# Both key/value heads of one branch in a prompt attention unit, with its matmul pairs in two halves of the array

## The reference

```python
# group B, per query block of 128 (w: sliding window, s: selected, c: compressed)
s_w = einsum('bqhgd,bkhd->bqhgk', q, kb) * SCALE          # h: 2 kv heads, g: 4 query heads of each
e, m, l = masked_exp(s_w, okw)
o_w = einsum('bqhgk,bkhd->bqhgd', normalise(e, l), vb)
out = g[..., 0] * o_c + g[..., 1] * o_s + g[..., 2] * o_w
```

## Time and profile before

| what | value |
| --- | --- |
| three runs, us | 1436.48, 1436.84, 1442.02 |
| the profiled execution, us | 1435.87 |
| its span, us | 1434.1 |
| mean granted PE clock | 0.947 of 2.4 GHz |
| PE busy | 1321.0 us, 92% of the span |
| DVE, ACT busy | 802.1 us (56%), 520.5 us (36%) |
| attention units, layer 0 and 1 | 363.7 to 452.2 us, 1060.2 to 1148.6 us |

### The profile page before, as it was taken

How to read it: one execution, slowest core, us unless ns; L and a number is a source line. 1 busy time by engine, 2 the same in 40 slices (tenths; PEclk the granted TensorE clock), 3 DMA queues, 4 the chain that set the end, 5 groups by cost and what they waited for, 6 DMA issues and landing times.

```text
span 1434.1 us, 24304 instructions
## 1 busy us (share of the span) xinstructions
PE 1321.0 (92%) x9753; PEld 1163.5 (81%) x9753; DVE 802.1 (56%) x1483; ACT 520.5 (36%) x762; POOL 118.4 (8%) x207
## 2 busy tenths in 40 slices
PE   5999997999998989999799999799899987999993
PEld 4999996656775789999799999766477666999992
DVE  5555546774665265554565544577547545555433
ACT  3333335410453263333353333334025434333321
POOL 9000002012000010000200000200120001000001
PEclk9999998997899989999989999899969998999996
DMA  8555577447164336646735546764632631565540
GB/s 260 180 181 167 148 209 256 144 147 244 46 176 119 93 110 185 190 132 162 217 121 178 175 132 173 237 240 133 206 127 73 163 117 60 177 187 167 155 108 30
DMA packets 251909, 226.81 MB, mean 158 GB/s; under 512 B 11716, under 2 KB 234066, under 8 KB 249634
## 3 DMA queue, kind: packets, MB, share of 16 engines
q1 hardware_dynamic: 245282, 204.08, 48.1%
q0 software_dynamic: 6528, 21.37, 4.3%
HBM read 221.55 MB, written 3.86 MB: 157 GB/s over the span
## 4 chain that ended last, share of the span: by engine, by line
PE 84%; DVE 9%; ACT 3%; issue 2%; DMA 1%; SPq 1%; POOL 0%; DVEq 0%
PE bank L746 21%; PE bank L747 21%; PE bank L748 21%; PE bank L665 9%; PE bank L855 3%; PE bank L1012 2%; PE bank L755 1%; PE bank L933 1%; PE bank L756 1%; PE bank L883 1%; PE bank L835 1%; DVE bc_pages L1656 1%; ACT x L1227 1%; DVE rstd L1755 1%; DVE w_low L1510 1%
## 5 line engine op out<-in xcount | busy, mean ns | idle before, releaser
L746 PE MATMUL bank<-x_high,w_low 128*128 128x264 f32 x1408 | 406.1, 288 | 27.6 <-DVE x_low L1492 23.3
L747 PE MATMUL bank<-x_low,w_high 128*128 128x264 f32 x1408 | 403.1, 286 | 0.0
L748 PE MATMUL bank<-x_high,w_high 128*128 128x264 f32 x1408 | 402.6, 286 | 0.0
L1510 DVE TENSOR_TENSOR w_low<-weights,w_high 128x2048 fp32r<-128x2048 f32 (+1 forms) x172 | 347.7, 2039 | 69.5 <-ACT w_high L1206 55.9
L746 PEld LDWEIGHTS bank<-x_high,w_low 128*128 128x128 f32 x1408 | 268.8, 191 | 31.6 <-issue 27.9
L747 PEld LDWEIGHTS bank<-x_low,w_high 128*128 128x128 f32 x1408 | 269.8, 192 | 0.0
L748 PEld LDWEIGHTS bank<-x_high,w_high 128*128 128x128 f32 x1408 | 268.3, 191 | 0.0
L746 PE MATMUL bank<-hidden_high,w_low 128*128 128x264 f32 x704 | 205.0, 291 | 0.0
L748 PE MATMUL bank<-hidden_high,w_high 128*128 128x264 f32 x704 | 199.8, 284 | 0.0
L747 PE MATMUL bank<-hidden_low,w_high 128*128 128x264 f32 x704 | 199.2, 283 | 0.0
L1248 ACT ACTIVATE w_high<-weights 128x2048 fp32r<-128x2048 f32 (+1 forms) x88 | 163.9, 1862 | 8.2 <-DMA weights<-in_ffn_wu_dram 8.2
(11 more groups left out here) (302 smaller groups left out, 1686.8 us busy)
## 6 DMA issues: line engine op xcount, KB each, us to landing
weights<-in_ffn_wg_dram SPq DMA_DIRECT2D x44, 1024.0 KB, 5.5
weights<-in_ffn_wu_dram SPq DMA_DIRECT2D x44, 1024.0 KB, 8.0
weights<-in_ffn_wd_dram SPq DMA_DIRECT2D x64, 704.0 KB, 6.3
weights<-in_w_in_dram SPq DMA_DIRECT2D x20, 1024.0 KB, 5.5
bc_pages<-in_cache_bc_kv_dram SPq DMA_DIRECT2D x128, 128.0 KB, 2.1
weights<-in_w_out_dram SPq DMA_DIRECT2D x16, 512.0 KB, 8.3
weights<-in_cache_bw_kv_dram SPq DMA_DIRECT2D x16, 256.0 KB, 3.3
ring<-in_cache_bw_kv_dram SPq DMA_DIRECT2D x16, 256.0 KB, 3.2
```

The source lines that it names most:

```text
L746: mm(out, w_low, v_high, start=start, stop=False)
L747: mm(out, w_high, v_low, start=False, stop=False)
L748: return mm(out, w_high, v_high, start=False, stop=stop)
L1510: tt(low(k, half), raw(k, half), high(k, half).bitcast(F32), ALU.subtract).then_inc(low_done, 1)
```

## The change

In group B a unit is now one branch with both key/value heads (for u = 2, 4, ... the selected branch, for u = 3, 5, ... the window), in group A the two heads of one `feats` row. So the two score matmuls of a unit read partitions 0 to 63 and 64 to 127, and they write two banks, 5 and 6; DVE waits for each of them. The value matmuls write output partitions 0 to 63 and 64 to 127, in turn. The numbers of matmuls, masks, exponentials and copies, and their sizes, stay as they are. Since a unit takes both banks, `scores(n + 2)` waits until unit n + 1 is masked (before: unit n). PE's loop has `values(n - 1)` first and `scores(n + 2)` after the hook.

```diff
 def scores(n):
-    out = bank_s((masked, first + n + 1))[:, :].rearrange("p (b n) -> p b n", b=2)
+    if first + n:
+        pe.wait_ge(masked, first + n)
+    q, key = (u, 2 + u) if u < 2 else (4 + (u - 2) // 2, 8 + (u - 2) % 2)
     for i in range(2):
-        if u < 2:
-            a, q, key = u * HD, i, 2 + i
-        else:
-            a, q, key = ((u - 2) % 2) * HD, 4 + (u - 2) // 2, 8 + i
-        last = part(out[:, i, 0:nk], feats[a:a + HD, q, q_cols], feats[a:a + HD, key, 0:nk],
-                    start=(i == 0), stop=(i == 1))
-    last.then_inc(s_full, 1)
+        half = slice(i * HD, (i + 1) * HD)
+        out = bank_s((masked, first + n + 1))
+        last = part(out[:, 0:nk], feats[half, q, q_cols], feats[half, key, 0:nk], start=True, stop=True)
+        last.then_inc(s_full, 1)
...
 def values(n):
...
-    for i, base in enumerate((BS, BW)):
-        for kt in range(qb + 1):
-            m = i * (qb + 1) + kt
-            v = base + P + kv * HD
-            last = part(out[kv * HD:(kv + 1) * HD, 0:P], tokens[:, kt, v:v + HD],
-                        pt[:, m * P:(m + 1) * P], start=False, stop=(i == 1 and kt == qb))
+    for kt in range(qb + 1):
+        for i in range(2):
+            m = i * (qb + 1) + kt
+            half = slice(i * HD, (i + 1) * HD)
...
+                v = (BS, BW)[branch] + P + i * HD
+                last = part(out[half, 0:P], tokens[:, kt, v:v + HD],
+                            pt[:, m * P:(m + 1) * P], start=False, stop=(branch == 1 and kt == qb))
...
 for n in range(BLOCKS):
     if n == UNITS - 2:
         cmp_scores(1)
+    if n:
+        values(n - 1)
+    hook(n)
     if n + 2 < BLOCKS:
         scores(n + 2)
-    hook(n)
     turn(n)
-    if n:
-        values(n - 1)
...
 def mask_unit(n):
-    ps = bank_s()[:, :].rearrange("p (b n) -> p b n", b=2)[:, :, 0:nk]
     for i in range(2):
-        last = ttr(probs[:, r, i, 0:nk], ps[:, i, :], m, ...
+        last = ttr(probs[:, r, i, 0:nk], bank_s()[:, 0:nk], m, ...
```

More of the change, by code:

```diff
@@ L944, in values @@
                         pe.wait_ge(pv_free, (first + n) // 2)
-                    if u < 2:
+                    g, branch = (u - 2) // 2, (u - 2) % 2
+                    if u >= 2 and branch == 0:
+                        part(out[:, 0:P], vcmp[0:HD, g * P:(g + 1) * P], pc_t[0:HD, :], start=True, stop=False)
+                    for kt in range(qb + 1):
                         for i in range(2):
-                            for kt in range(qb + 1):
-                                m = i * (qb + 1) + kt
[L949 to L956, removed]
-                    for i, base in enumerate((BS, BW)):
-                        for kt in range(qb + 1):
-                            m = i * (qb + 1) + kt
-                            v = base + P + kv * HD
-                            last = part(out[kv * HD:(kv + 1) * HD, 0:P], tokens[:, kt, v:v + HD],
-                                        pt[:, m * P:(m + 1) * P], start=False, stop=(i == 1 and kt == qb))
+                            m = i * (qb + 1) + kt
+                            half = slice(i * HD, (i + 1) * HD)
+                            if u < 2:
+                                v = AV + (2 * u + i) * HD
+                                last = part(out[half, u * P:(u + 1) * P], tokens[:, kt, v:v + HD],
+                                            pt[:, m * P:(m + 1) * P], start=(kt == 0), stop=(kt == qb))
+                            else:
+                                v = (BS, BW)[branch] + P + i * HD
+                                last = part(out[half, 0:P], tokens[:, kt, v:v + HD],
+                                            pt[:, m * P:(m + 1) * P], start=False, stop=(branch == 1 and kt == qb))
                     last.then_inc(pv_done, 1)
@@ L1838, in mask_unit @@
                     for i in range(2):
-                        last = ttr(probs[:, r, i, 0:nk], ps[:, i, :], m, -SCALE, -MASKED, ALU.add, ALU.min,
+                        last = ttr(probs[:, r, i, 0:nk], bank_s()[:, 0:nk], m, -SCALE, -MASKED, ALU.add, ALU.min,
                                    stat[:, (first + n) % 4, i:i + 1])
@@ L1848, in norm_unit @@
                     if u >= 2:
-                        h = ((u - 2) % 2) * 4 + (u - 2) // 2
-                        step(tt(row[:, 4:6], row[:, 4:6], gates[:, qb, 3 * h + 1:3 * h + 3], ALU.mult))
+                        g, branch = (u - 2) // 2, (u - 2) % 2
+                        gate = gates[:, qb, :].rearrange("p (k g t) -> p k g t", k=2, g=4)[:, :, g, 1 + branch]
+                        step(tt(row[:, 4:6], row[:, 4:6], gate, ALU.mult))
                     nk = (qb + 1) * P
```

## The result

| | before | after |
| --- | --- | --- |
| median of 5 runs beside each other, us | 1437.65 | 1449.13 |
| lowest and highest, us | 1436.48, 1442.02 | 1448.14, 1451.62 |
| span of the profiled execution, us | 1434.1 | 1446.4 |
| units of layer 0, first compressed score to first square sum (L844), us | 94.7 | 98.7 |
| the same in layer 1, us | 94.9 | 101.7 |

The ratio is 1.0075, with a 95% interval of 1.0055 to 1.0094. The time is 9.1 us above the predicted 1440.0, inside the range of 1432 to 1452, and the kernel is measurably slower where no change was held likeliest. Of the 12.3 us by which the span grew, 4.0 lie in layer 0's units, 6.8 in layer 1's, 1.1 between them, and 0.3 ahead of layer 0's units.

What follows compares the result with a forecast made beforehand. PE's own groups were taken to bound the units. Per layer -12.9 (pairs) + 13.5 (copy waits) + 3.0 (longer waits) - 2.2 (DVE waits) = +1.4, both layers +2.8: 1440 us, range 1432 to 1452.

Steps and rivals of the forecast that it cites:

- What the pairs save: PE's score and value groups, both halves: column or row halves run beside each other, saving 12.9 us a layer.
- What the copy's and the longer waits cost: PE before values: waits for ACT's copy, 13.5 us a layer; longer ones at values 2, 6, 4, 8, 18, 3.0.
- What goes: PE's waits for DVE's normalisation before turns 11, 13, 17 and 19 vanish, 2.2 us a layer; scores' mask wait costs nothing.
- the second half's compressed scores: On PE ahead of values 7: taken to cover part of their copy wait, 0.7 us together with values 10's cover.
- the clock: Rival, second half of the units: gaps lower PE's granted clock, streaming doubles, 13 us a layer, 1466 us; chance 0.05.
- The forecast's +2.8: Whole kernel: net change of savings and waits over both layers, +1.4 us each.
- The forecast's own range: Whole kernel: 1434 to 1447 us, for 0.1 us on each of 40 waits and longer waits 3 us a layer off.
- the milder half of the one-kind rival: PE's score and value groups: part of the pairs' saving is missing, up to 1452; whole rival's chance 0.12.
- One kind only, or three turns out of four: Rival, PE's score and value groups: half of 25.8 us saving missing, 1452.5 us; no overlap at all 1465; chance 0.12.
- PE going past waiting values: Rival, PE's unit loop: PE takes hook or scores behind waiting values, so 13.5 and 3.0 fall away, 1411 us; chance 0.05.

Runs made afterwards that it cites:

- order alone: Kernel before with only the changed kernel's group order (values n - 1, hook, scores n + 2, turn n), no pairs: 1470.07 us, ratio 1.0246.
- the old place with its transfers first: Changed kernel with values n - 1 back behind turn n and the eight big window transfers issued before the 24 small ones: 1417.45 us, ratio 0.9845.

## Why the prediction was right, and where its size was off

- **What the pairs save: right.** Both kinds overlap fully: 0.59 and 0.63 us in the second half, 0.37 and 0.42 in the first, against 1.02, 1.06, 0.58 and 0.64. Forecast 25.8 us; order alone against the changed kernel gives 20.9 by the medians and 25 by the ratios, the old place with its transfers first against before about 22. In layer 0 the units lost 4.0 us; with the waits below taken off, 11.4 of the 12.9 remain, and 0.5 of the missing 1.5 is the first key transposes at half clock (3.61 for 3.14 us from start to start). In layer 1, with the two slow stretches taken off as well, 12.2 remain, and those transposes took 3.11 for 3.05 us.
- **What the copy's and the longer waits cost: right.** 15.2 us of idle time, and some 0.07 us of overlap with the group ahead lost at each of 20 values groups, 16.6 us (17.0 in layer 1); forecast 13.5 + 3.0 = 16.5. Values 2 stood 1.90 and values 6 1.36 us, for the reasons given; values 18 1.18.
- **What goes: right.** The turns' 2.2 us. The scores' wait for the mask shows once a layer, 0.48 us ahead of scores 1, and the wait for DVE behind it is shorter by more (0.41 for 1.08 us, in layer 1 0.64 for 1.43).
- **The first step that failed: the second half's compressed scores.** They were taken as cover for values 7, and cover they were. But in the new order both score banks hold unit 9 by then, so they wait for its mask: 0.94 us and the lost overlap, 1.0 us a layer, 2.0 in all, costed at nothing.
- **The second: the clock.** It was a rival with one size, the whole second half at 1.2 GHz for 13 us a layer, and given 0.05 on the strength of two windows that had kept 1.00. It came in stretches of 3.4 and 6.8 us, which cost 3.2 us in layer 1's units, 1.0 behind layer 0's, and 0.5 and 0.1 at the two heads, 4.8 us in the profiled execution. The forecast itself had no term for a few short stretches.
- **Together.** The forecast's +2.8, 0.6 for the somewhat longer waits ahead of the values, 2.0 for the compressed scores and 4.8 for the clock make 10.2 of the 12.3 us by which the span grew. Some 1.0 us of the pairs' saving in layer 0, 0.7 in layer 1 and 0.3 us ahead of the units stay unexplained.
- **The range: in part luck.** The forecast's own range ended at 1447, and 1449.13 lies above it. It is the margin for the milder half of the one-kind rival, up to 1452, that holds the result, and that rival is refuted.
- **The rivals.** One kind only, or three turns out of four: refuted by the lengths. PE going past waiting values: refuted, it stood at 19 of the 20 values groups of a layer (values 7 come behind the compressed scores, which wait themselves). Slower by the clock: right in kind, far smaller.

## What to carry to other kernels

Time taken off the bounding engine shows only as far as nothing else is due: put the consumer of a copy a whole group behind it, and look up the next floor (here a list of transfers issued one by one, that lay just under the old time) before a gain is booked. In these kernels idle time on PE seems to have a price beyond itself, through the granted clock; allow for a few stretches at the lower level wherever a change turns PE work into waiting. An edit that takes one more buffer at a time can add a wait for every user of these buffers, those outside the loop too: here the compressed scores.

## What was not expected of the hardware

- Value records of two column halves overlap even when they are not neighbours: group length 0.59 us with either order, in starts 12 ns apart (that each pair is one record of each half is inferred).
- Useless transposes inside a wait made a kernel faster, 1429.89 to 1426.05 us, with a mean granted clock of 0.9465 for 0.9437.
- Shortening the waits by 1.4 us a layer left the time as it was (ratio 1.0084 for 1.0075); in the profiled execution more stretches at 1.2 GHz came, in other places.
